# A fused transformer layer on one core: rows of v follow rows of u of the same tile by 24 beats, and the input projection runs beside the routing

## The chip, the core and the metric

One Trainium2 chip, one of its cores. The metric is the device time of one launch in microseconds; lower is better. The kernel is compared before and after one change.

## What is computed

One layer of a transformer is applied to a prompt of 1024 tokens and to 64 sample tokens (8 sequences of 8), width 1024, all in float32. For every token:

```python
qa, ka, va, qb, kb, vb, ga, gb = split(rms_norm(h, norm_mix) @ w_in)      # w_in: 1024 x 5120
o_a, o_b = attend(...)                  # branch A: difference of two softmax maps, branch B: stick-breaking
h = h + (sigmoid(ga) * (rms(o_a) @ w_proj_diff) + sigmoid(gb) * (o_b @ w_proj_sb)) @ w_out
xb = rms_norm(h, norm_ffn)
s = (xb @ w_q) against 8 heads x 2 x 128 sub-keys; top 16 of each half; top 16 of their sums -> idx, g
act = gelu(einsum('td,thkd->thk', xb, u_tab[idx]))                        # 128 rows of u for each token
h = h + einsum('thk,thkd->td', g * act, v_tab[idx])                       # 128 rows of v for each token
y = rms_norm(h, norm_final)
```

The outputs are y for prompt and sample and the keys and values of both branches. The two tables u_tab and v_tab have 16384 rows of 1024 floats. Each token takes 128 rows from each: this is most of what the kernel moves.

## The kernel before

**Stages.** A first stage makes the bias slabs and projects the first two tiles (a tile is 128 tokens, one for each partition). It ends at about 196 us. All that follows is the main stage, and the change touches only this.

**Turns and beats.** The main stage is one list of beats, written out in advance. A turn is 128 beats (`BEATS`), and in turn t the kernel attends, merges and routes for tile t (tiles 0 to 7 are the prompt, tile 8 the sample; functions `pe_piece`, `act_piece`, `dve_piece`). Beats 0 to 61 of a turn are attention. Beats 62 (`MERGE_AT`) to 84 are the merge: 24 weight blocks of 512 KB are read in order and multiplied. Beats 85 (`KEYS_AT`) to 125 are the routing, nearly all of it on VectorE, and end in the list of indices (`choose`) and the softmax gates (`gate`). TensorE, ScalarE, VectorE and GpSimd each walk the same list with a program of their own and meet at semaphores. So a wait of one engine at beat b holds all of its later beats.

**The rows.** One indirect DMA on GpSimd's queue (`pool_gather`, L1162) brings one row of u or v for each of 128 tokens, 512 KB, into one of nine places of `ring`. A place is used again once the row in it has been consumed. A row of u is multiplied with the token and summed on VectorE (`dve_dot`, L1899). A row of v is added with its weight either on VectorE (`dve_add`, L1917) or on TensorE, by a matrix product with a diagonal that ScalarE makes four beats ahead (`act_diag` L1564, `pe_add` L1388), into banks 0 and 1 of PSUM. `v_on_dve` says which. Rows of u of tile e pass in turn e+1 from beat 6 (`ULAG`); rows of v of tile e pass in turn e+2 from beat 14 (`VLAG`). In between stands one gelu over all 128 dots of the tile (L1581, turn e+2 beat 6) and one product with the gates (`dve_weights`, L1924, beat 9). The sample has 64 rows of each. The last beat is 1357.

**The end of a tile.** `dve_join` (L1930) adds the banks to the sum on VectorE, `act_finish` (L1602) and `dve_finish` (L1938) normalise it. `acc` holds three such sums.

**The projection.** Tiles 2 to 8 are projected beside the main stage, in 70 units (ten column blocks of w_in for seven tiles) of four quarters each (`pe_quarter`, L1375: two 128x512 products, four records in the trace). Each quarter has its beat: 81 in turn 0 (43 of them at beats 85 to 127), 116 in turn 1 and 83 in turn 2, at two a beat. All units of a column block follow one another, so that its weights (four loads of 512 KB, issued by ScalarE) are read once. Units go to banks 0 and 1 by turns; ScalarE takes them out and stores them (`act_quarter`, L1548). `sync_attend` and the `keys` piece of turn 3 wait until all quarters are done.

Of the kernel before, what the change touches and what calls it, by code (L numbers as in the profile page):

```python
# [48 lines left out]
R = 9  # L49
# [4 lines left out]
VLAG = 14  # L54
# [4 lines left out]
B_END = 48  # L59
# [35 lines left out]
def build(nc, a, o):  # L95
# [20 lines left out]
    with ctx:  # L116
# [138 lines left out]
        B_CHUNKS = (1, 2, 0, 4, 5, 3, 6, 7, 8, 9)  # L255
        B_UNITS = [(c, t) for c in B_CHUNKS for t in B_TILES]
# [32 lines left out]
        with ExitStack() as stage:  # L289
# [61 lines left out]
            with nc.Block() as block:  # L351
# [13 lines left out]
                def _(sp):  # L365
# [9 lines left out]
                    for j in range(4):  # L375
                        sp.dma_start(b_weights(j), b_source(B_CHUNKS[0], j)).then_inc(s_bw[j], 16)
# [219 lines left out]
        with ExitStack() as stage:  # L596
# [8 lines left out]
            acc = sb("t_acc", [P, 3, D])  # L605
# [194 lines left out]
            def row_at(beat, turns, lag):  # L800
                e, s = divmod(beat - lag, BEATS)
                return (e - turns, s) if 0 <= e - turns <= NPT and s < slots_of(e - turns) else None

            def u_at(beat):
                return row_at(beat, 1, ULAG)

            def v_at(beat):
                return row_at(beat, 2, VLAG)

            LAST_BEAT = (NPT + 2) * BEATS + VLAG + slots_of(NPT)  # L810

            def v_on_dve(e, s):

                n = slots_of(e)
                turn, b = divmod((e + 2) * BEATS + VLAG + s, BEATS)
                if (turn, b) < (FIRST, B_END):

                    return True
                if s < 3 or s >= n - 3:
                    return True  # L820
                if turn > NPT:
                    return s % 2 == 0 if b > ULAG + NS or turn > NPT + 1 else s % 3 == 0
# [118 lines left out]


            NQ = 4 * len(B_UNITS)
            quarter_beats = [b for b in range(2, MERGE_AT, 2)] + [b for b in range(MERGE_AT, KEYS_AT, 3)] + [b for b in range(KEYS_AT, BEATS)]
            quarter_beats += [BEATS + b for b in range(BEATS) if not MERGE_AT <= b < KEYS_AT or b % 2]
            left_over = NQ + 2 - len(quarter_beats)
            quarter_beats += [FIRST * BEATS + n // 2 for n in range(left_over)]
            assert quarter_beats[-1] < FIRST * BEATS + B_END
            quarters = {}
            for n, b in enumerate(quarter_beats):  # L950
                quarters.setdefault(b, []).append(n)

# [64 lines left out]
            def sync_attend(sp, t):  # L1017
                kw = width(t)
                if t >= FIRST:

                    if t >= 4:
                        sp.wait_ge(s_rmsy, t - 3)
# [29 lines left out]
                if t >= 3:  # L1052
                    sync_finish(sp, t - 3)
# [18 lines left out]
            def sync_finish(sp, e):  # L1072
                dst = y_out[1] if is_sample(e) else y_out[0][tile(e), :]
                sp.wait_ge(s_y_out, e + 1)
                sp.dma_start(dst, acc[0:out_rows(e), e % 3, :]).then_inc(s_yst, 16)

            def sync_sample(sp):
# [40 lines left out]
                for b in range(NB_DEC):  # L1118
# [13 lines left out]
                    if b == 3:  # L1132
                        sync_finish(sp, NPT - 3)
# [7 lines left out]
            def sync_program(sp):  # L1141
# [7 lines left out]
                for e in range(NPT - 2, NPT + 1):  # L1149
                    sync_finish(sp, e)  # L1150
# [46 lines left out]
            def pe_scores(pe, t, u, hf):  # L1197
                kw = width(t)
                if u == 0 and t:

                    pe.wait_ge(s_scc, 2 * t)
                if u == 0 and hf == 0:
# [164 lines left out]
            def pe_quarter(pe, n):  # L1367

                unit, j = divmod(n, 4)
                c, t = B_UNITS[unit]  # L1370
                if j == 0 and unit >= 2:
                    pe.wait_ge(s_bev, unit - 1)
                pe.wait_ge(s_bw[j], 16 * (B_CHUNKS.index(c) + 1))
                for k in range(2):
                    m = nc.tensor.matmul(ps[0:height(t), unit % 2, :], xT_of(t, 2 * j + k, 2 * j + k + 1)[:, 0, :],  # L1375
# [3 lines left out]
            def pe_add(pe, e, s):  # L1379
                n = out_rows(e)  # L1380
                if v_first(e, s):

                    pe.wait_ge(*((s_yc, e) if e else (s_bev, len(B_UNITS))))
# [8 lines left out]
            def pe_program(pe):  # L1392
                for beat in range(LAST_BEAT):
# [5 lines left out]
                    for n in quarters.get(beat, ()):  # L1399
                        if n < NQ:  # L1400
                            pe_quarter(pe, n)
                pe.wait_ge(s_fold, 1)
                pe.wait_ge(s_vsum, v_ends(NPT, True))
                for c in range(2):
                    m = nc.tensor.matmul(ps[0:NS, c, :], fold[:], acc[:, NPT % 3, c * CH:(c + 1) * CH], start=False, stop=True)
# [16 lines left out]
            def act_piece(act, t, kind, *which):  # L1422
# [113 lines left out]
            def act_quarter(act, n):  # L1536

                unit, j = divmod(n - 1, 4)
                if 0 <= unit < len(B_UNITS):
                    c, t = B_UNITS[unit]  # L1540
                    if t == B_TILES[-1] and c != B_CHUNKS[-1]:
                        act.wait_ge(s_bq, n)
                        act.dma_start(b_weights(j), b_source(B_CHUNKS[B_CHUNKS.index(c) + 1], j)).then_inc(s_bw[j], 16)
                    if j == 3:
                        act.wait_ge(s_bq, n)
                        if unit >= 2:
                            act.wait_ge(*stored(*B_UNITS[unit - 2]))
                        nc.scalar.copy(b_out(unit % 2)[0:height(t)], ps[0:height(t), unit % 2, :]).then_inc(s_bev, 1)  # L1548
                unit, j = divmod(n - 2, 4)
                if 0 <= unit < len(B_UNITS) and j == 3:  # L1550
                    c, t = B_UNITS[unit]
# [3 lines left out]
            def act_diag(act, e, s):  # L1555
                k = v_place[e, s]
                if v_first(e, s):
                    act.wait_ge(s_wgt, e + 1)
                    if is_sample(e):
                        act.wait_ge(s_fold, 1)  # L1560
# [6 lines left out]
            def act_program(act):  # L1567
                for beat in range(LAST_BEAT):
                    turn, b = divmod(beat, BEATS)
                    if b == ULAG and 1 <= turn <= NPT + 2:  # L1570
                        e = turn - 1
                        if e <= NPT and e != NPT - 1:

                            if e:
                                act.wait_ge(*dots_done(e - 1))
                            act.wait_ge(s_xn, e + 1)
                            nc.scalar.copy(both(4)[:, :], xn_of(e)).then_inc(s_xps, 1)
                        if e:
                            cols = slice(0, slots_of(e - 1))
                            act.wait_ge(*dots_done(e - 1))  # L1580
                            nc.scalar.activation(act_u[:, cols], dots[:, (e - 1) % 2, cols], ACT.Gelu).then_inc(s_gelu, 1)  # L1581
# [3 lines left out]
                    if b == VLAG and turn >= 3:  # L1585
                        act_finish(act, turn - 3)
# [3 lines left out]
                    for n in quarters.get(beat, ()):  # L1590
                        act_quarter(act, n)
                act.wait_ge(s_folded, 1)
                act_finish(act, NPT)

            def act_finish(act, e):
# [3 lines left out]
                else:  # L1599
                    act.wait_ge(s_yc, e + 1)  # L1600
                    src = acc[:, e % 3, :]
# [301 lines left out]
            def dve_add(dve, e, s):  # L1903
                total = acc[:, e % 3, :]
                if s == 0:
                    dve.wait_ge(s_h, e + 1)
                    dve.wait_ge(s_wgt, e + 1)
                if v_place[e, s]:
                    dve.wait_ge(s_vsum, v_place[e, s])
                dve.wait_ge(*arrived("v", e, s))  # L1910
# [10 lines left out]
            def dve_weights(dve, e):  # L1921
                cols = slice(0, slots_of(e))
                dve.wait_ge(s_gelu, e + 1)
                nc.vector.tensor_tensor(wgt[:, e % 2, cols], act_u[:, cols], gate[:, e % 2, cols], ALU.mult).then_inc(s_wgt, 1)  # L1924

            def dve_join(dve, e):
                total = acc[:, e % 3, :]
                dve.wait_ge(s_sum, v_ends(e, False))
                dve.wait_ge(s_vsum, v_ends(e, True))
# [78 lines left out]
```

## Time and profile before

| | |
|---|---|
| median of 3 runs | 4093.12 us (4084.87 to 4098.61) |
| profiled execution, its own time | 4105.51 us |
| its span, first to last instruction | 4103.7 us |
| TensorE busy | 3034.7 us (74%) |
| VectorE busy | 2650.3 us (65%) |
| GpSimd busy | 2373.0 us (58%) |
| ScalarE busy | 870.8 us (21%) |
| moved by DMA | 1390.19 MB, 339 GB/s over the span |

The profile is one execution. Its page gives busy times, a picture of the span in 40 slices, the chain of waits that ended last, and the costliest groups of instructions by line. Busy shares are means over stages with different limits, so the stretches below are cut at beats: the first row of u at a beat is taken from the trace (VectorE's instruction of L1899), and the time at which it starts is where that beat begins.

### The profile page before, as it was taken

What the parts mean: (1) busy time and instruction counts of PE and PEld (TensorE: products, weight loads), DVE (VectorE), ACT (ScalarE), POOL (GpSimd) and SP (SyncE); (2) the same over time, 40 slices, a digit from 0 to 9 for tenths busy, and PEclk for the clock granted to TensorE, in tenths of its full rate; (3) what the DMA queues carried; (4) which work ended last, traced back from release to release, by engine and by line L of the source; (5) the groups of instructions that cost most, each with busy time, mean ns of one, the idle gap of its engine ahead of it and who ended that gap; (6) DMA issues with size and microseconds to landing.
All of it is one profiled execution on the core that took longest, in us unless ns stands there. A gap on an engine that the chain in (4) does not pass through costs nothing.

```text
span 4103.7 us, 28498 instructions
## 1 busy us (share of the span) xinstructions
PE 3034.7 (74%) x7904; PEld 1357.0 (33%) x7904; DVE 2650.3 (65%) x5344; ACT 870.8 (21%) x1778; POOL 2373.0 (58%) x2218
## 2 busy tenths in 40 slices
PE   6899988987756776777677767776877687764566
PEld 4644433433223322332243234322432233321221
DVE  4214658675777576767676778676867665676544
ACT  4321211220122112211231123112311132111011
POOL 0100334465667566766676677656756676577776
PEclk9999999998988997889898988998989898997899
DMA  6543898899989998999899999998999999999998
GB/s 220 185 158 123 278 334 284 287 338 409 367 339 367 409 366 328 362 404 379 330 351 408 387 346 357 408 376 328 340 399 376 354 360 328 408 336 370 375 363 314
DMA packets 410545, 1390.19 MB, mean 339 GB/s; under 512 B 48493, under 2 KB 51565, under 8 KB 409197
## 3 DMA queue, kind: packets, MB, share of 16 engines
q0 software_dynamic: 316384, 1151.48, 74.5%
q1 hardware_dynamic: 74772, 200.96, 13.3%
q10 hardware_dynamic: 19232, 35.92, 2.4%
q8 instruction: 66, 1.08, 0.1%
q14 instruction: 91, 0.75, 0.0%
HBM read 1358.52 MB, written 29.66 MB: 338 GB/s over the span
## 4 chain that ended last, share of the span: by engine, by line
PE 25%; DMA 19%; POOL 16%; issue 14%; DVE 14%; another core or an unknown queue 4%; ACT 3%; SPq 0%; DVEq 0%; ACTq 0%; POOLq 0%
POOL t_ring L1162 16%; DMA t_ring<-in_peer_v,t_idx 11%; PE ps L1375 10%; PE ps L1388 5%; DVE t_ring L1899 5%; PE ps L1238 4%; DMA t_ring<-in_peer_u,t_idx 4%; DMA val<-in_w_in 2%; PE ps L1190 2%; DVE t_acc L1917 2%; PE ps L1215 1%; DMA t_big<-in_peer_w_query 1%; DMA t_big<-in_w_out 1%; DMA keyT<-in_cache_k_sb 1%
## 5 line engine op out<-in xcount | busy, mean ns | idle before, releaser
L1388 PE MATMUL ps<-t_ring,t_diag 128*128 128x512 f32 (+1 forms) x2696 | 1457.1, 672 | 613.9 <-DMA t_ring<-in_peer_v,t_idx 509.6
L1162 POOL DMA_INDIRECT t_ring<-in_peer_u,t_idx x1088 | 1153.9, 1061 | 1055.4 <-PE ps L1388 282.4
L1162 POOL DMA_INDIRECT t_ring<-in_peer_v,t_idx x1088 | 1199.5, 1102 | 497.7 <-issue 284.9
L1899 DVE CUSTOM_DVE_ANT_0 t_ring<-t_ring,ps 128x1024 f32<-128x1024 f32 x960 | 1158.2, 1214 | 379.4 <-DMA t_ring<-in_peer_u,t_idx 333.1
L1388 PEld LDWEIGHTS ps<-t_ring,t_diag 128*128 128x128 f32 (+1 forms) x2696 | 509.6, 207 | 1460.8 <-DMA t_ring<-in_peer_v,t_idx 886.6
L1917 DVE SCALAR_TENSOR_TENSOR t_acc<-t_ring,t_wgt,t_acc 128x1024 f32<-128x1024 f32 x413 | 531.1, 1286 | 194.5 <-DMA t_ring<-in_peer_v,t_idx 163.5
L1238 PE MATMUL ps<-t_big,t_pTr 128*128 128x512 f32 x864 | 428.1, 641 | 92.5 <-DMA t_big<-in_w_out 24.6
L1564 ACT ACTIVATE t_diag<-ident,t_wgt 128x128 f32<-128x128 f32 x645 | 248.9, 400 | 893.2 <-PE ps L1388 489.3
L1375 PE MATMUL ps<-val,keyT 128*128 128x512 f32 x800 | 368.8, 604 | 29.6 <-DMA val<-in_w_in 28.5
L1416 ACT COPY t_pTr<-ps 128x512 f32<-128x512 f32 (+3 forms) x216 | 111.1, 514 | 800.9 <-PE ps L1190 525.2
L1238 PEld LDWEIGHTS ps<-t_big,t_pTr 128*128 128x128 f32 x864 | 166.6, 203 | 338.1 <-issue 187.1
L1375 PEld LDWEIGHTS ps<-val,keyT 128*128 128x128 f32 x800 | 149.2, 193 | 200.6 <-issue 168.2
L1899 DVE CUSTOM_DVE_ANT_0 t_ring<-t_ring,t_xn_sb 128x1024 f32<-128x1024 f32 x128 | 156.1, 1221 | 53.1 <-DMA t_ring<-in_peer_u,t_idx 48.8
L1215 PE MATMUL ps<-keyT,t_big 128*128 128x512 f32 (+3 forms) x384 | 169.7, 556 | 22.1 <-DVE t_mx L1628 10.0
L1190 PE MATMUL ps<-ident,t_big 128*128 128x128 f32 x576 | 101.7, 291 | 100.3 <-ACT t_pTr L1416 40.6
L1628 DVE CUSTOM_DVE_ANT_0 t_big<-ps,t_big 128x128 f32<-128x128 f32 (+7 forms) x64 | 48.4, 756 | 178.9 <-PE ps L1215 85.7
L1375 PE MATMUL ps<-val,xT_end 128*128 128x512 f32 (+1 forms) x320 | 144.9, 596 | 0.0
L1228 PEld LDWEIGHTS ps<-val,t_pTr 128*128 128x128 f32 x864 | 119.9, 206 | 69.5 <-issue 59.0
L1190 PEld LDWEIGHTS ps<-ident,t_big 128*128 128x128 f32 x576 | 72.1, 150 | 177.8 <-issue 93.0
L1228 PE MATMUL ps<-val,t_pTr 128*128 128x64 f32 (+1 forms) x864 | 117.4, 284 | 15.7 <-ACT t_pTr L1416 8.3
L1215 PEld LDWEIGHTS ps<-keyT,t_big 128*128 128x128 f32 x384 | 75.3, 214 | 94.8 <-issue 79.7
L1548 ACT COPY val<-ps 128x512 f32<-128x512 f32 (+1 forms) x70 | 41.0, 586 | 304.8 <-PE ps L1375 290.3
(215 smaller groups left out, 2177.8 us busy)
## 6 DMA issues: line engine op xcount, KB each, us to landing
t_big<-in_w_out SPq DMA_DIRECT2D x72, 512.0 KB
t_big<-in_peer_w_query SPq DMA_DIRECT2D x72, 512.0 KB
wraw<-in_w_in SPq DMA_DIRECT2D x40, 512.0 KB, 5.9
t_big<-in_w_proj_diff SPq DMA_DIRECT2D x36, 512.0 KB
val<-in_w_in ACTq DMA_DIRECT2D x36, 512.0 KB
t_big<-in_w_proj_sb SPq DMA_DIRECT2D x36, 512.0 KB
t_ring<-in_peer_u,t_idx POOLq DMA_INDIRECT x1088
t_ring<-in_peer_v,t_idx POOLq DMA_INDIRECT x1088
```

The lines of the kernel that those rows point to most:

```text
L1162: pool.indirect_dma_start(row(kind, e, s), None, table, bass.IndirectOffsetOnAxis(ap=idx[:, e % 3, s:s + 1], axis=0)).then_inc(s_ring[g % ...
L1190: m = nc.tensor.transpose(ps[:, 6, k * P:k * P + n], blk, ident[0:n, 0:n])
L1215: m = nc.tensor.matmul(scores_of(t, hf)[:, c:c + wide], qz[:, u, hf, :], keyT[:, u, c:c + wide], start=True, stop=True)
L1228: m = nc.tensor.matmul(ps[:, 7, col:col + wide], pTr[:, kb, :], val[:, kb, u * P + hf * 64:u * P + hf * 64 + wide], start=(kb == 0), stop= ...
L1238: m = nc.tensor.matmul(ps[:, 2 + c, :], pTr[:, k, :], wring[:, w % 4, c * CH:(c + 1) * CH], start=(k == blocks[0]), stop=(k == blocks[1] - 1))
L1375: m = nc.tensor.matmul(ps[0:height(t), unit % 2, :], xT_of(t, 2 * j + k, 2 * j + k + 1)[:, 0, :], b_weights(j)[:, k, :], start=(j == 0 and ...
L1388: m = nc.tensor.matmul(ps[0:n, c, :], diag[:, v_place[e, s] % NDG, 0:n], row("v", e, s)[:, c * CH:(c + 1) * CH], start=v_first(e, s), stop ...
L1416: act_T.raised_by(nc.scalar.copy(dst, src))
L1564: nc.scalar.activation(diag[:, k % NDG, 0:out_rows(e)], unit[:], ACT.Copy, scale=wgt[:, e % 2, s:s + 1]).then_inc(s_diag, 1)
L1628: nc.vector.tensor_tensor_reduce(out=z_of(u)[:, hf, 0:kw], in0=scores_of(t, hf), in1=bias[:, u % 2, 0:kw], scale=1.0, scalar=LOWEST, op0=A ...
L1899: nc.vector.tensor_tensor_reduce(out=row("u", e, s), in0=row("u", e, s), in1=x_row, scale=1.0, scalar=0.0, op0=ALU.mult, op1=ALU.add, accu ...
L1917: m = nc.vector.scalar_tensor_tensor(out=total, in0=row("v", e, s), scalar=wgt[:, e % 2, s:s + 1], in1=total, op0=ALU.mult, op1=ALU.add)
```

## The change

The four numbers and the planning of beats change, and what hangs on them:

- Rows of v of tile e pass in turn e+1, 24 beats behind the rows of u of the same tile. They were a turn and eight beats behind. The last beat is 1245 in place of 1357.
- Gelu and the product with the gates are made for groups of 16 rows, two and three beats after the group's last dot.
- `acc` holds two sums in place of three, and `ring` has ten places in place of nine.
- Quarters: 64 in turn 0 (26 of them from beat 85), 112 in turn 1, 104 in turn 2, the last at beat 116. Between beats 85 and 127 of turns 1 and 2 they go to banks 2 and 3, since banks 0 and 1 then hold the sum of v; at each passage from one pair of banks to the other the first quarter waits.
- The column blocks 6 to 9 come first for tile 2 alone and then for tiles 3 to 8, so each is read twice: 14 sets of weights in place of 10.
- Rows of v in turn 1, and in turn 2 up to beat 84, are added on VectorE, but for two of three at beats 85 to 123 of turn 1. The join of tile 0 stands at beat 2 of turn 2, that of a later tile at beat 30 of the next turn but one.

```diff
-R = 9
+R = 10
-VLAG = 14
+VLAG = 24
+GROUP = 16
+JOIN_0 = 2
-        B_CHUNKS = (1, 2, 0, 4, 5, 3, 6, 7, 8, 9)
-        B_UNITS = [(c, t) for c in B_CHUNKS for t in B_TILES]
+        B_GROUPS = [(c, B_TILES) for c in (1, 2, 0, 4, 5, 3)]
+        B_GROUPS += [(c, B_TILES[:1]) for c in (6, 7, 8, 9)] + [(c, B_TILES[1:]) for c in (6, 7, 8, 9)]
+        B_UNITS = [(c, t) for c, tiles in B_GROUPS for t in tiles]
...
-            acc = sb("t_acc", [P, 3, D])
+            acc = sb("t_acc", [P, 2, D])
...
             def v_at(beat):
-                return row_at(beat, 2, VLAG)
+                return row_at(beat, ULAG + VLAG)
+            def group_at(beat, lag):
+                row = row_at(beat, ULAG + GROUP - 1 + lag)
+                return (row[0], row[1] // GROUP) if row and row[1] % GROUP == 0 else None
+            def weighed(e, g):
+                return e * (NSLOT // GROUP) + g + 1
-            LAST_BEAT = (NPT + 2) * BEATS + VLAG + slots_of(NPT)
+            LAST_BEAT = (NPT + 1) * BEATS + ULAG + VLAG + slots_of(NPT)
...
+            quarter_beats = [b for b in range(2, MERGE_AT, 2)] + [b for b in range(MERGE_AT, KEYS_AT, 3)] + [b for b in range(KEYS_AT, KEYS_AT + 26)]
+            quarter_beats += [BEATS + b for b in range(MERGE_AT)] + [BEATS + b for b in range(MERGE_AT + 1, MERGE_AT + 20, 2)]
+            quarter_beats += [BEATS + b for b in range(KEYS_AT, KEYS_AT + 40)]
+            quarter_beats += sorted([2 * BEATS + b for b in range(JOIN_0 + 1, MERGE_AT)] + [2 * BEATS + b for b in (20, 30, 40)])
+            quarter_beats += [2 * BEATS + b for b in range(MERGE_AT + 1, MERGE_AT + 20, 2)] + [2 * BEATS + b for b in range(KEYS_AT, KEYS_AT + 32)]
+            def bank_of(unit):
+                return 2 * beside_routing(unit) + unit % 2
...
             def v_on_dve(e, s):
...
-                if (turn, b) < (FIRST, B_END):
-                    return True
+                if turn == 1 or e == 0 or (turn == 2 and b < KEYS_AT):
+                    return not (turn == 1 and KEYS_AT <= b < BEATS - 4) or s % 3 == 0
...
-                return b < MERGE_AT and s % 3 == 0
+                return (b < MERGE_AT or turn == 2) and s % 3 == 0
...
             def pe_quarter(pe, n):
+                if j == 0 and beside_routing(unit) and not beside_routing(unit - 2):
+                    pe.wait_ge(s_scc, 2 * turn + 2)
+                if j == 0 and unit >= 2 and beside_routing(unit - 2) and not beside_routing(unit):
+                    pe.wait_ge(s_yc, 1)
...
+            def act_gelu(act, e, g):
+                cols = slice(g * GROUP, (g + 1) * GROUP)
+                act.wait_ge(s_dot, e * NSLOT + (g + 1) * GROUP)
+                if e:
+                    act.wait_ge(s_wgt, weighed(e - 1, g))
+                nc.scalar.activation(act_u[:, cols], dots[:, e % 2, cols], ACT.Gelu).then_inc(s_gelu, 1)
...
-            def dve_weights(dve, e):
-                cols = slice(0, slots_of(e))
-                dve.wait_ge(s_gelu, e + 1)
+            def dve_weights(dve, e, g):
+                cols = slice(g * GROUP, (g + 1) * GROUP)
+                dve.wait_ge(s_gelu, weighed(e, g))
                 nc.vector.tensor_tensor(wgt[:, e % 2, cols], act_u[:, cols], gate[:, e % 2, cols], ALU.mult).then_inc(s_wgt, 1)
...
+                    if group_at(beat, 2):
+                        act_gelu(act, *group_at(beat, 2))
...
-                    if b == ULAG + 3 and 2 <= turn:
-                        dve_weights(dve, turn - 2)
+                    if group_at(beat, 3):
+                        dve_weights(dve, *group_at(beat, 3))
```

## Rows read from the trace of the kernel before

**Rows 1.** The page: busy times by engine; DMA's rate in 40 slices.

```profile
PE 3034.7 (74%) x7904; PEld 1357.0 (33%) x7904; DVE 2650.3 (65%) x5344; ACT 870.8 (21%) x1778; POOL 2373.0 (58%) x2218
...
GB/s 220 185 158 123 278 334 284 287 338 409 367 339 367 409 366 328 362 404 379 330 351 408 387 346 357 408 376 328 340 399 376 354 360 328 408 336 370 375 363 314
```

**Rows 2.** Busy time by stretch: us, each engine's busy us (instructions), PE clock, DMA share, GB/s.

```profile
1566.10:1980.10 414.00, 292.85 (x744) 131.22 (x744) 290.79 (x591) 89.22 (x192) 269.38 (x256) 0.88 0.96 368
3909.30:4062.40 153.10, 101.57 (x203) 30.26 (x204) 75.55 (x62) 22.14 (x57) 114.54 (x105) 0.96 0.97 367
4062.40:4103.70 41.30, 19.22 (x34) 4.28 (x32) 15.56 (x13) 2.10 (x5) 20.75 (x16) 0.84 0.65 225
```

**Rows 3.** The chain that ended last, 384 to 760 us: start, us, what.

```profile
383.76 29.33 PE ps L1375 x68
...
659.89 15.36 DMA val<-in_w_in
675.29 38.19 PE ps L1375 x88
```

**Rows 4.** VectorE in order of time, 378 to 430 us: start, us, instruction.

```profile
384.52 0.29 DVE L1832 TENSOR_TENSOR t_gate<-t_gexp,t_grec 128x128 f32<-128x128 f32 x1
418.37 0.43 DVE L1628 CUSTOM_DVE_ANT_0 t_big<-ps,t_big 128x256 f32<-128x256 f32 x1 [33.55 <-PE ps L1215]
```

**Rows 5.** As rows 2: turn 1 from beat 30, cut at beats 62, 85, 127.

```profile
474.00:537.20 63.20, 59.10 (x168) 27.01 (x167) 43.25 (x81) 11.82 (x25) 30.02 (x32) 1.00 0.90 334
537.20:612.80 75.60, 60.23 (x146) 25.76 (x145) 32.91 (x51) 8.00 (x13) 20.01 (x23) 0.95 0.88 321
612.80:725.00 112.20, 98.79 (x244) 42.05 (x242) 92.74 (x299) 13.79 (x21) 47.70 (x43) 0.98 0.85 294
725.00:751.10 26.10, 23.54 (x61) 10.73 (x60) 10.28 (x26) 6.68 (x13) 7.52 (x8) 1.00 0.75 285
```

**Rows 6.** As rows 2: turn 2 from beat 6, cut at beats 30, 62, 85.

```profile
751.10:842.30 91.20, 89.97 (x251) 40.28 (x249) 59.83 (x105) 25.17 (x54) 46.65 (x40) 1.00 0.85 292
842.30:947.40 105.10, 81.30 (x208) 35.93 (x207) 72.86 (x103) 16.85 (x36) 68.03 (x62) 0.89 0.94 353
947.40:1035.80 88.40, 69.00 (x168) 30.08 (x166) 56.49 (x71) 11.82 (x22) 51.76 (x48) 0.92 1.03 408
1035.80:1159.00 123.20, 85.54 (x169) 29.40 (x168) 95.65 (x298) 18.82 (x45) 83.06 (x83) 0.97 0.96 362
```

**Rows 7.** As rows 2: turn 3 and the boundary before it, the same cuts.

```profile
1159.00:1190.90 31.90, 18.25 (x44) 8.39 (x42) 14.31 (x27) 8.14 (x15) 15.66 (x16) 0.73 0.71 267
1190.90:1262.60 71.70, 44.55 (x135) 21.96 (x136) 59.76 (x106) 27.58 (x61) 53.09 (x48) 0.87 0.97 376
1262.60:1357.10 94.50, 66.30 (x167) 29.71 (x166) 60.84 (x92) 16.89 (x37) 65.09 (x65) 0.83 0.98 377
1357.10:1447.30 90.20, 64.85 (x166) 27.83 (x164) 56.47 (x70) 13.42 (x25) 49.67 (x49) 0.98 1.03 408
1447.30:1570.40 123.10, 90.63 (x167) 31.48 (x168) 95.54 (x298) 17.21 (x42) 83.95 (x82) 0.92 0.96 358
```

**Rows 8.** The costliest groups: a row of v added on VectorE.

```profile
L1917 DVE SCALAR_TENSOR_TENSOR t_acc<-t_ring,t_wgt,t_acc 128x1024 f32<-128x1024 f32 x413 | 531.1, 1286 | 194.5 <-DMA t_ring<-in_peer_v,t_idx 163.5
```

**Rows 9.** ScalarE in order of time around a gelu, 744 to 760 us.

```profile
750.01 1.02 ACT L1577 COPY ps<-t_xn_sb 128x1024 f32<-128x1024 f32 x1
...
751.05 1.28 ACT L1581 ACT_TABLE_LOAD   x1
752.34 0.31 ACT L1581 ACTIVATE t_act_u<-t_dots 128x128 f32<-128x128 f32 x1
752.67 1.28 ACT L1441 ACT_TABLE_LOAD   x1
```

**Rows 10.** GpSimd's waits in turn 4: who for whom, us in total, times, longest.

```profile
POOL t_ring L1162 <- issue: 65.0, 209, 1.1
POOL t_ring L1162 <- PE ps L1388: 50.4, 15, 11.3
POOL t_ring L1162 <- remote: 20.3, 9, 3.5
```

More of the change, by code:

```diff
@@ L798, in slots_of, with row_at @@
                 return NSLOT // 2 if e == NPT else NSLOT
-            def row_at(beat, turns, lag):
-                e, s = divmod(beat - lag, BEATS)
-                return (e - turns, s) if 0 <= e - turns <= NPT and s < slots_of(e - turns) else None
+            def row_at(beat, lag):
+                e, s = divmod(beat - BEATS - lag, BEATS)
+                return (e, s) if 0 <= e <= NPT and s < slots_of(e) else None
             def u_at(beat):
-                return row_at(beat, 1, ULAG)
+                return row_at(beat, ULAG)
@@ new lines, in build, with beside_routing @@
+            quarter_beats += [2 * BEATS + b for b in range(MERGE_AT + 1, MERGE_AT + 20, 2)] + [2 * BEATS + b for b in range(KEYS_AT, KEYS_AT + 32)]
+            assert len(quarter_beats) == NQ
+            quarters = {}
+            for n, b in enumerate(quarter_beats):
+                quarters.setdefault(b, []).append(n)
+            def beside_routing(unit):
+                turn, b = divmod(quarter_beats[4 * unit], BEATS)
+                ends = divmod(quarter_beats[4 * unit + 3], BEATS)
+                assert not turn or (turn, b >= KEYS_AT) == (ends[0], ends[1] >= KEYS_AT)
+                return turn > 0 and b >= KEYS_AT
@@ L939, in build @@
                 at(KEYS_AT + 40, "gate", of=pieces)
[L943 to L951, printed above, removed]
             def unit_of(c, t):
@@ L1148, in sync_program @@
                 sync_weights(sp, NPT)
-                for e in range(NPT - 2, NPT + 1):
+                for e in range(NPT - 1, NPT + 1):
                     sync_finish(sp, e)
@@ L1556, in act_diag @@
                 k = v_place[e, s]
[L1557 to L1560, printed above, removed]
+                if s == min(r for r in range(s // GROUP * GROUP, slots_of(e)) if not v_on_dve(e, r)):
+                    act.wait_ge(s_wgt, weighed(e, s // GROUP))
+                if v_first(e, s) and is_sample(e):
+                    act.wait_ge(s_fold, 1)
                 if k >= NDG:
@@ L1569, in act_program @@
                     turn, b = divmod(beat, BEATS)
-                    if b == ULAG and 1 <= turn <= NPT + 2:
+                    if b == ULAG and 1 <= turn <= NPT + 1 and turn != NPT:
                         e = turn - 1
[L1572 to L1577, printed above, removed]
                         if e:
-                            cols = slice(0, slots_of(e - 1))
                             act.wait_ge(*dots_done(e - 1))
-                            nc.scalar.activation(act_u[:, cols], dots[:, (e - 1) % 2, cols], ACT.Gelu).then_inc(s_gelu, 1)
+                        act.wait_ge(s_xn, e + 1)
+                        nc.scalar.copy(both(4)[:, :], xn_of(e)).then_inc(s_xps, 1)
+                    if group_at(beat, 2):
+                        act_gelu(act, *group_at(beat, 2))
                     ahead = v_at(beat + DIAG_AHEAD)
@@ L1589, in act_program @@
                         act_piece(act, t, *piece)
-                    for n in quarters.get(beat, ()):
+                    for n in quarters.get(beat - 2, ()):
+                        act_store(act, n)
+                    for n in quarters.get(beat - 1, ()):
                         act_quarter(act, n)
```

111 lines of the change are left out of this document (64 added, 47 removed).

## Prediction

> **What bounds the kernel now.** I read the page first: no engine is above 74%, but from turn 2 on DMA moves 340 to 409 GB/s in nearly every slice, against 158 to 334 in the slices before [rows 1]. Then I cut the span at beats. In turn 4, a steady one, 256 rows pass in 414.0 us, 1.62 us a row, with DMA at 0.96 and 368 GB/s [rows 2]. The merge of turn 3 runs at 408 GB/s with DMA's share at 1.03 [rows 7]; I take 408 as the roof. At it the 152 MB of a steady turn (414.0 x 368) would take 373 us, so a turn is transfer with some 40 us of gaps, and rows cost about the same wherever they stand, if the engines keep up.
>
> The two ends are different. From beat 62 of turn 9 on 152 rows are left and almost nothing stands beside them: 105 pass in 153.1 us, 1.46 us each [rows 2]. At the other end turn 1 has one row a beat, and DMA is not full: 334, 321, 294 and 285 GB/s [rows 5]. There the chain of waits runs through quarters on TensorE, not through rows: 68 records of L1375 in 29.33 us, 88 in 38.19 [rows 3]. Four records are a quarter: 1.73 us. So the kernel is bound by TensorE in turns 0 to 2 and by transfer after that, and the change moves 112 rows from the second kind of stretch to the first: 98 into turn 1, 14 into turn 2, all off the end.
>
> **End of turn 0.** VectorE finishes the gates at 384.8 us and has nothing until 418.4: 33.55 us for the scores of tile 1 [rows 4], and in that time the chain holds 68 records, 17 quarters, in 29.33 us [rows 3]. These are the backlog: 43 quarters stand at beats 85 to 127. The change leaves 26, just 17 fewer. TensorE would be done at 383.8 and VectorE waits for the short chain of transposes alone. Removed: **-29**. This is no transfer-bound stretch, so nothing else is late next; the 17 return below.
>
> **The end.** Beats from 62 of turn 9 on: 40 rows in place of 152. 112 x 1.46 = **-163**. The last 41.3 us with their sums and stores [rows 2] stay.
>
> **Turn 1.** For each stretch I take the traffic it had, add 0.524 MB for each new row and divide by the rate that turn 3 shows at the same beats; then I look whether an engine needs more. A row of v costs VectorE 1.29 us [rows 8]; on TensorE it has the same two products as a quarter, 1.73.
> - Beats 6 to 30: no row of v, the same quarters: 0.
> - 30 to 62: 63.2 us x 334 = 21.1 MB, plus 32 rows (16.8) = 37.9, at 377 [rows 7] 100 us. VectorE 43.3 + 32 x 1.29 = 85, TensorE 59 [rows 5]. 100: +37.
> - 62 to 85: 24.3 + 12.1 = 36.3 MB at 408: 89 us, +13. TensorE has one quarter less.
> - 85 to 127: 33.0 MB + 42 rows (22.0) + eight extra weight loads (4.2: units 42 and 43 are alone in their groups) = 59.2. At 358 [rows 7] 165 us, at 408 145. TensorE 98.8 + 26 rows - 2 quarters = 140; VectorE 92.7 + 17 x 1.29 = 115. 152, between the two rates, nearer the roof as this mix has big loads: +40.
> - 127 to 6: 31.9 as in turn 3 [rows 7], and 2 for weights: +8.
>
> Sum **+98**. The rest of GpSimd's queue behind these rows is only more rows.
>
> **Turn 2.**
> - 6 to 30: TensorE 90.0 - 23 quarters (40) = 50. VectorE 59.8 + 8 x 1.29 = 70. Traffic 26.6 MB + 8 rows (4.2) + eight loads (4.2) - 3.6 for 23 quarters' weights and stores = 31.4, at 376 84 us: -7 [rows 6, 7].
> - 30 to 62: 11 quarters more, 10 rows fewer on TensorE (83 us), VectorE 86; traffic 37.1 + 1.7 = 38.8 MB at 377: 103: -2.
> - 62 to 85: 36.1 + 1.6 MB at 408: +4.
> - 85 to 127: 44.6 + 4.9 MB, 121 to 138 us; TensorE 85.5 + 32 quarters - 14 rows = 117; VectorE 95.7 + 14 x 1.29 = 114. 134: +11.
>
> Sum **+6**. That the last quarter comes at beat 116, and SyncE's loads for turn 3 stand behind it, leaves about 12 beats at 2.95 us, 35 us, for 1 MB; cost nothing. If the quarters run that late, all of turn 3 starts later, one to one.
>
> Bounds for both turns together: with 408 GB/s in every stretch about 45 less, +60. With nothing hidden, each moved row and quarter paid on its engine one after the other: turn 1 72 x 1.29 + 26 x 1.73 less 4 quarters, plus 8.4 MB at 377, +153; turn 2 (37 rows more on VectorE, 29 fewer and 30 quarters more on TensorE) +50. So +60 to +203; I take +104, since TensorE and VectorE stay under the transfer time in all stretches.
>
> **Steady turns, 3 to 8.** The same 256 rows, the same shares of the engines. Two small terms.
>
> *Gelu in groups.* The trace has one per tile: table load 1.28, gelu 0.31, and then 1.28 again for the table of exp [rows 9]. The seven more bring by my reading of the beats some seven loads and seven gelus, 10.6 us of ScalarE a turn, which has 89 of 414 busy [rows 2]. Behind ScalarE's wait stand its copies for TensorE's transposes and the diagonals; behind VectorE's wait for the gelu stand the dots that free the ring. VectorE has two beats of its own work between the last dot and the product, TensorE four beats after that, and a beat lasts 2.95 us (94.5 / 32 [rows 7]). Bounds: 0, and all 10.6. The product on 16 columns is not in the trace; below the 0.28 of 128. I take +3 a turn. The Trainium skill, page "ScalarE: Activation LUTs", section "What ACT_TABLE_LOAD costs", gives 1.28 us for the load and 1.38 more for a drain, 2.66 for each switch. The trace agrees on the load and shows no drain: copy until 751.03, load at 751.05, gelu at 752.34, next load at 752.67 [rows 9]. By the page ScalarE would have 20 us more a turn, by the rows 10.6.
>
> *The tenth place.* GpSimd issues a row when a place is free. In turn 4 it waits 15 times for TensorE, 50.4 us in all, and 9 times for something unseen, 20.3 us [rows 10]. With one place more, one more row is under way at each such wait. 24 x 1.46 = 35 us is the upper bound, 0 the lower; what is full at 408 gives nothing back, and the longest wait, 11.3 us, is mended by an eighth. I take -6.
>
> Together -3 a turn, six turns: **-18**.
>
> **Sum.** -29 - 163 + 98 + 6 - 18 = -106. The span goes from 4103.7 to 3998, the execution's own time from 4105.5 to 3999.5. The median of the runs was 4093.12, 0.9970 of that execution: 3987 us.
>
> **The rivals.**
>
> *The ring gives more.* If half of the 35 us of each steady turn comes back and the gelus cost nothing, -17 a turn in place of -3: another 84, 3903 us. For it: the waits are few and long. Against: the floor of 373 us a turn, and that a place more doesn't make TensorE's own waits shorter. 0.10.
>
> *The first turns take it all.* If in turns 1 and 2 nothing is hidden, +203 meets -192 and the steady terms take off what is left: 4086 us, with the steady terms at nothing 4104; no change. For it: in turn 1 TensorE is at 94% of beats 30 to 62 and VectorE waits on it for each score; five changes of weights follow one another at units 41 to 46, and the chain showed 15.36 us for such a load [rows 3], where four beats are 12. Against: 74 to 123 GB/s of unused rate there [rows 5]. 0.12.
>
> *Slower: each group of 16 stops the ring.* VectorE must have a group's gelu before it goes on, ScalarE must have the dots before it copies anything for TensorE. If the load, the gelu and the load back (2.87 us [rows 9]) show in full for each of the 59 added gelus, that is +169: -29 - 163 + 104 + 169 = +81, 4174 us. It decides from 88 / 59 = 1.5 us a group on, about one load and the gelu. For it: ScalarE is already held for long stretches in its own order. Against: the beats between, and that rows wait for transfer anyway. 0.13. By the page's switch of 2.66 us the group would cost 5.6 us, +332, 4335 us; the trace agrees only with the load of 1.28.
>
> **How the numbers follow.** My forecast, 3987, has 0.62, with a range of its own of 3935 to 4040 from the bounds of the first two turns and of the steady terms; the rivals 0.10, 0.12 and 0.13, 0.03 for the rest. The range of 3900 to 4085 leaves out the slower rival, a part of the no-change one, and the fastest tail. Within 0.3% (12 us) is what a measurement of this kernel can hardly tell from no change. Faster: 0.62 + 0.10 + half of the second rival, 0.78. Same 0.08, slower 0.14.
>
> **What would show it.** In the trace after: the wait of VectorE before tile 1's first scores shrinks from 33.6 us to under 8. Turn 1 lasts about 425 us from beat 6 to beat 6, not 324, with DMA at 360 or more from beat 30; turn 2 about 445. Turns 3 to 7 keep 409 to 414 us. From beat 62 of turn 9 to the end 70 us in place of 233. Wrong it would be if VectorE's or TensorE's rows show waits for ScalarE's gelu of over 1.5 us each, if turn 1 is over 500 us, or if steady turns move by over 10 us.

## The result, and the profile after

The kernel after the change takes 3972.07 us (median of four runs, 3960.66 to 3981.93). The kernel before, on the same chip, takes 4088.99 us (four runs, 4071.45 to 4098.61). The ratio is 0.9718, with a 95% interval of 0.9673 to 0.9763: 2.8% faster. The forecast was 3987 us, with a chance of 0.78 for faster. The profiled execution took 3976.95 us, its span 3975.2.

The page after the change, busy times and DMA's rate in 40 slices, beside [rows 1]:

```profile
PE 2933.8 (74%) x7680; PEld 1324.0 (33%) x7680; DVE 2721.1 (68%) x5459; ACT 923.5 (23%) x1836; POOL 2399.5 (60%) x2218
...
GB/s 217 201 143 128 339 410 407 397 406 410 409 374 361 387 402 354 344 375 408 365 337 347 409 388 323 348 404 407 311 358 386 377 344 384 356 359 354 344 375 323
```

TensorE has 101 us less to do and VectorE 71 more: 56 rows of v went from the one to the other. What matters is DMA's rate in the fifth to tenth slices: 278, 334, 284, 287, 338 and 409 GB/s before, 339, 410, 407, 397, 406 and 410 now.

VectorE in order of time, after, between the gates of tile 0 and the first scores of tile 1 (start, us, instruction, in brackets the idle time before it):

```profile
385.02 0.29 DVE L1880 TENSOR_TENSOR t_gate<-t_gexp,t_grec 128x128 f32<-128x128 f32 x1
391.31 0.42 DVE L1676 CUSTOM_DVE_ANT_0 t_big<-ps,t_big 128x256 f32<-128x256 f32 x1 [6.00 <-PE ps L1245]
```

The wait of 33.55 us [rows 4] is 6.00.

Busy time by stretch, after; the columns are those of [rows 2]. The first five lines are turn 1 from beat 6, cut at beats 30, 62, 85 and 127 as in [rows 5]; the next five are turn 2 with the same cuts, as [rows 6] and the first line of [rows 7]; then turn 4 as in [rows 2]; then beats 30 to 62 of turn 9, and all that follows:

```profile
399.60:452.50 52.90, 47.50 (x139) 22.27 (x138) 38.20 (x91) 18.09 (x47) 21.79 (x24) 1.00 0.86 316
452.50:556.50 104.00, 82.55 (x219) 36.59 (x217) 83.44 (x115) 18.83 (x35) 71.09 (x64) 0.92 1.01 390
556.50:640.10 83.60, 61.35 (x148) 27.12 (x149) 62.67 (x77) 10.24 (x18) 50.84 (x47) 0.87 1.03 409
640.10:775.90 135.80, 122.01 (x286) 49.26 (x284) 114.91 (x318) 22.76 (x47) 92.43 (x85) 0.99 1.02 399
775.90:802.20 26.30, 14.40 (x27) 6.30 (x28) 21.29 (x32) 6.77 (x10) 15.73 (x15) 0.74 1.03 406
802.20:879.20 77.00, 60.53 (x171) 28.59 (x170) 68.29 (x114) 21.14 (x49) 51.66 (x46) 0.93 1.03 408
879.20:983.90 104.70, 79.37 (x207) 35.00 (x206) 86.79 (x117) 23.24 (x39) 72.70 (x66) 0.87 1.03 408
983.90:1071.90 88.00, 69.51 (x164) 29.86 (x162) 62.71 (x78) 10.31 (x18) 50.34 (x47) 0.90 1.03 410
1071.90:1200.30 128.40, 113.22 (x248) 45.25 (x248) 112.05 (x316) 20.65 (x47) 89.42 (x83) 0.95 0.99 382
1200.30:1229.20 28.90, 18.75 (x46) 8.59 (x46) 13.24 (x26) 9.11 (x17) 15.45 (x16) 0.76 0.78 300
...
1637.00:2050.40 413.40, 288.25 (x746) 128.77 (x745) 291.63 (x597) 99.22 (x206) 272.13 (x257) 0.89 0.96 369
3817.40:3905.10 87.70, 46.03 (x75) 11.90 (x76) 58.18 (x85) 10.65 (x28) 63.22 (x62) 0.79 1.01 389
3905.10:3975.20 70.10, 38.22 (x70) 9.33 (x68) 31.81 (x35) 6.77 (x18) 37.59 (x37) 0.85 0.77 290
```

Read the last number of each line. From beat 62 of turn 1 to beat 85 of turn 2 all stretches but one stand at 406 to 410 GB/s with DMA's share at 1.03, where before they had 285 to 353 (408 in the merge of turn 2 alone). The one is turn 1's beats 85 to 127, at 399 GB/s. So these 515 us stand at or near the roof. The whole account, between the same beats:

| stretch | before | after | change | forecast |
|---|---|---|---|---|
| up to the first row of u | 427.0 | 399.6 | -27.4 | -29 |
| turn 1 | 324.1 | 402.6 | +78.5 | +98 |
| turn 2 | 439.8 | 427.0 | -12.8 | +6 |
| turns 3 to 8 | 2524.0 | 2521.2 | -2.8 | -18 |
| turn 9, beats 6 to 62 | 155.9 | 154.7 | -1.2 | 0 |
| from there to the end | 232.9 | 70.1 | -162.8 | -163 |
| sum | 4103.7 | 3975.2 | -128.5 | -106 |

(A turn goes from its beat 6 to the next turn's.)

### The profile page after: what moved, and what is told of

It reads as the page before. It is cut to its first block, busy times and chain, and to the rows that moved or that the text cites. A ratio compares the mean times of both kernels' runs of the same rounds, so it can differ in the third digit from the quotient of the medians.

```text
span 3975.2 us, 28361 instructions
## 1 busy us (share of the span) xinstructions
PE 2933.8 (74%) x7680; PEld 1324.0 (33%) x7680; DVE 2721.1 (68%) x5459; ACT 923.5 (23%) x1836; POOL 2399.5 (60%) x2218
## 4 chain that ended last, share of the span: by engine, by line
DMA 21%; PE 19%; POOL 19%; issue 15%; DVE 14%; ACT 3%; another core or an unknown queue 3%; SPq 0%; DVEq 0%; ACTq 0%; POOLq 0%
POOL t_ring L1189 19%; DMA t_ring<-in_peer_v,t_idx 13%; PE ps L1268 6%; DVE t_ring L1947 5%; PE ps L1428 5%; PE ps L1412 3%; DMA t_ring<-in_peer_u,t_idx 3%; DMA t_big<-in_w_out 2%; DMA t_big<-in_peer_w_query 2%; PE ps L1217 2%; DVE t_acc L1968 2%; PE ps L1245 1%; DMA keyT<-in_cache_k_sb 1%; PE ps L1258 1%
## 5 line engine op out<-in xcount | busy, mean ns | idle before, releaser
L1428 PE MATMUL ps<-t_ring,t_diag 128*128 128x512 f32 (+1 forms) x2472 | 1338.3, 672 | 516.5 <-DMA t_ring<-in_peer_v,t_idx 442.1
L1189 POOL DMA_INDIRECT t_ring<-in_peer_u,t_idx x1088 | 1209.5, 1112 | 682.8 <-issue 268.2
L1189 POOL DMA_INDIRECT t_ring<-in_peer_v,t_idx x1088 | 1170.4, 1076 | 713.7 <-issue 310.0
L1428 PEld LDWEIGHTS ps<-t_ring,t_diag 128*128 128x128 f32 (+1 forms) x2472 | 467.1, 206 | 1255.8 <-DMA t_ring<-in_peer_v,t_idx 740.2
L1968 DVE SCALAR_TENSOR_TENSOR t_acc<-t_ring,t_wgt,t_acc 128x1024 f32<-128x1024 f32 x469 | 603.6, 1287 | 152.6 <-DMA t_ring<-in_peer_v,t_idx 125.8
L1268 PE MATMUL ps<-t_big,t_pTr 128*128 128x512 f32 x864 | 440.7, 655 | 113.1 <-DVE t_big L1750 43.8
L1412 PE MATMUL ps<-val,keyT 128*128 128x512 f32 x800 | 390.0, 624 | 57.9 <-DMA val<-in_w_in 46.5
L1605 ACT ACTIVATE t_diag<-ident,t_wgt 128x128 f32<-128x128 f32 x583 | 222.7, 398 | 577.4 <-PE ps L1428 294.0
L1245 PE MATMUL ps<-keyT,t_big 128*128 128x512 f32 (+3 forms) x384 | 161.7, 534 | 23.4 <-issue 10.2
```

The costliest lines, as they stand in the source:

```text
L1189: pool.indirect_dma_start(row(kind, e, s), None, table, bass.IndirectOffsetOnAxis(ap=idx[:, e % 3, s:s + 1], axis=0)).then_inc(s_ring[g % ...
L1245: m = nc.tensor.matmul(scores_of(t, hf)[:, c:c + wide], qz[:, u, hf, :], keyT[:, u, c:c + wide], start=True, stop=True)
L1268: m = nc.tensor.matmul(ps[:, 2 + c, :], pTr[:, k, :], wring[:, w % 4, c * CH:(c + 1) * CH], start=(k == blocks[0]), stop=(k == blocks[1] - 1))
L1412: m = nc.tensor.matmul(ps[0:height(t), bank_of(unit), :], xT_of(t, 2 * j + k, 2 * j + k + 1)[:, 0, :], b_weights(j)[:, k, :], start=(j == ...
L1428: m = nc.tensor.matmul(ps[0:n, c, :], diag[:, v_place[e, s] % NDG, 0:n], row("v", e, s)[:, c * CH:(c + 1) * CH], start=v_first(e, s), stop ...
L1605: nc.scalar.activation(diag[:, k % NDG, 0:out_rows(e)], unit[:], ACT.Copy, scale=wgt[:, e % 2, s:s + 1]).then_inc(s_diag, 1)
```

## The experiments

All change the kernel after. The first four were compared with the kernel before on one chip, the last three on another. The kernel after itself was not run on the second chip, so the last three are held against it by their ratios to the kernel before; spans of theirs are compared across chips.

**The same kernel again**, as the base for the others.

> The changed kernel again, timed on the chip of the three runs beside it, as what they are held against. All theories: 0.972 of the kernel before.

Measured: 3966.99 us, ratio 0.9702 (0.9683 to 0.9721), span 3965.2. Up to the first row of u 401.1, turn 1 401.5, turn 2 435.0, turns 3 to 8 2502.1, the end 68.8. So the account above repeats within 2 us, but for turn 2, which moves by 8 between two profiles of one kernel, and the sum of turns 3 to 8, which moves by 19. A difference of some us a steady turn can't be read from two profiles; for that the ratios must serve.

**Nine places in the ring again.**

```diff
-R = 10
+R = 9
```

> The changed kernel with nine places in the ring in place of ten. Turns 3 to 8 came out only 2.8 us shorter in all, where I had forecast 18. Theory A (two real terms that cancel: the tenth place gives 6 us a turn or more, the gelus in groups take nearly as much): 6 us a turn and about 50 us in all slower than the changed kernel. Theory B (the tenth place gives next to nothing, since the waits of the ring come from engines that stand still longer than a row's pace): under 10 us in all.

Measured: 3974.72 us, ratio 0.9704 (0.9682 to 0.9725), as without the edit. Turn 4 lasts 412.3 us with ten places, 409.9 with nine. GpSimd's waits in that turn, ten places (who for whom, us in total, times, longest):

```profile
POOL t_ring L1189 <- issue: 67.8, 214, 1.8
POOL t_ring L1189 <- PE ps L1428: 39.2, 14, 9.3
POOL t_ring L1189 <- DVE t_dots L1947: 14.8, 19, 3.7
POOL t_ring L1189 <- remote: 14.3, 7, 3.3
```

The same view with nine:

```profile
POOL t_ring L1189 <- issue: 74.0, 229, 2.6
POOL t_ring L1189 <- PE ps L1428: 37.6, 11, 9.2
POOL t_ring L1189 <- remote: 13.0, 5, 3.3
POOL t_ring L1189 <- DVE t_dots L1947: 11.5, 13, 3.3
```

Apart from "issue" that is 68.3 us with ten places and 62.1 with nine, in as long a turn. A place more does not shorten the waits for a consumer. The 6 us a turn that I took for it would be 36 us here; the ratios differ by 0.0002, 1 us, with an interval of some 11 us to either side for the difference. The rival "the ring gives more" falls with them.

**Groups of eight**, twice the gelus and more changes of table.

```diff
-GROUP = 16
+GROUP = 8
```

> Groups of 8 rows in place of 16: 68 more gelus, with their table loads where another function stands between, 64 more products with the gates. Theory A (each added gelu takes 0.4 us of the time, as 3 us a turn for seven): 25 to 30 us slower. Theory B (ScalarE's idle time hides them): within 10 us of the changed kernel. The slower rival of the prediction (2.87 us for each gelu): 190 us slower.

Measured: 3963.65 us, ratio 0.9701 (0.9680 to 0.9722): no change. ScalarE's groups of instructions for the gelu, groups of 16 (count, busy us, mean ns, idle us before):

```profile
L1640 ACT ACT_TABLE_LOAD x48 | 61.6, 1283 | 6.8 <-PE ps L1412 5.3 <-ACT val L1587 0.5 <-issue 0.3
...
L1640 ACT ACTIVATE t_act_u<-t_dots 128x16 f32<-128x16 f32 x68 | 14.6, 215 | 102.8 <-DVE t_dots L1947 64.7 <-issue 24.0 <-remote 13.4
```

And groups of eight:

```profile
L1640 ACT ACT_TABLE_LOAD x72 | 92.4, 1283 | 4.6 <-PE ps L1412 2.3 <-issue 0.7 <-ACT val L1587 0.4
...
L1640 ACT ACTIVATE t_act_u<-t_dots 128x8 f32<-128x8 f32 x136 | 28.3, 208 | 211.5 <-DVE t_dots L1947 115.5 <-issue 69.9 <-remote 22.4
```

The line charges ScalarE with 44.5 us more (30.8 for the loads, 13.7 for the gelus). With 15 more loads on other lines ScalarE as a whole is busy 983.4 us in place of 922.3, and the median is 3 us shorter. The slower rival needed 1.5 us for each added group, 102 us for these 68; it is refuted. One thing is easier here than in the kernel after: a group of eight leaves ten beats between its product with the gates and its first diagonal, a group of 16 two. Two more things to see. Only 48 of 68 gelus, and 72 of 136, had to load the table: the others found it in place. And ScalarE idles 102.8 and 211.5 us before its gelus, most of it for the last dot of the group: the gelu is early, not late. VectorE's product with the gates, which needs the gelu, shows no wait for it in the kernel after (idle before the 68 products, us and times):

```profile
L1975 DVE TENSOR_TENSOR t_wgt<-t_act_u,t_gate x68: 151/164/224, 435.9 to 3933.9; 128x16 f32<-128x16 f32 x68
...
  issue: 1.0, 2
```

**The backlog back in turn 0**: 16 quarters from beats 101 to 116 of turn 2 into beats 111 to 126 of turn 0; each quarter between takes an earlier beat.

```diff
-... + [b for b in range(KEYS_AT, KEYS_AT + 26)]
+... + [b for b in range(KEYS_AT, KEYS_AT + 42)]
...
-... + [2 * BEATS + b for b in range(KEYS_AT, KEYS_AT + 32)]
+... + [2 * BEATS + b for b in range(KEYS_AT, KEYS_AT + 16)]
```

> The changed kernel, but 42 quarters at the routing beats of turn 0 in place of 26, as nearly as before the change, and 16 fewer at the routing beats of turn 2. Theory A (the backlog of TensorE holds tile 1's first scores, and in turn 2 the quarters lie beside transfer): VectorE's first row of u comes 16 x 1.73 = 28 us later, turn 2's beats 85 to 127 shorten by 0 to 8 us, total 20 to 28 us slower. Theory B (a quarter costs its 1.73 us wherever it stands): no change in all.

Measured: 3982.63 us, ratio 0.9734 (0.9711 to 0.9757), 13 us slower than its base by the ratios (with some 12 to either side), 20.8 by the spans. The first row of u comes at 426.1 us, not 401.1. Busy time by stretch, with the backlog: turn 1 beats 6 to 30, turn 2 beats 85 to 127:

```profile
426.10:471.60 45.50, 45.50 (x139) 23.41 (x138) 38.20 (x91) 17.89 (x47) 21.75 (x24) 1.00 0.90 306
...
1094.40:1220.40 126.00, 90.95 (x184) 35.54 (x184) 112.06 (x317) 17.71 (x42) 88.68 (x82) 0.89 0.97 368
```

The same stretches of the base:

```profile
401.10:452.90 51.80, 48.72 (x139) 22.87 (x138) 38.22 (x91) 18.19 (x47) 21.77 (x24) 0.97 0.88 322
...
1072.80:1202.80 130.00, 115.48 (x247) 44.85 (x245) 112.29 (x317) 20.12 (x45) 91.09 (x84) 0.93 0.99 376
```

Look at the last: TensorE has 24.5 us less to do there, and the stretch is 4.0 us shorter. In turn 0 sixteen quarters cost 25.0 us, 1.56 each. Within turn 1, where the quarters only take earlier beats, gains and losses cancel (401.1 us in place of 401.5): beats 85 to 127 last 143.5 us for 135.5. A quarter is at nearly its full price where all wait for it and nearly free where rows are being transferred. That is the first term of the forecast, confirmed by undoing it.

**The transposes of the keys ahead.** A steady turn begins with a gap that the forecast passed over: from beat 127 to beat 6 DMA has 267 GB/s in [rows 7] and 300 after the change. TensorE in order of time there, base kernel, the start of turn 5:

```profile
2026.43 0.60 PE L1217 MATMUL ps<-ident,gain_mix 128*128 128x128 f32 x4
2034.45 1.12 PE L1217 MATMUL ps<-ident,gain_mix 128*128 128x128 f32 x4 [7.43 <-ACT keyT L1455]
```

ScalarE at the same time:

```profile
2033.81 0.58 ACT L1455 COPY keyT<-ps 128x512 f32<-128x512 f32 x1 [17.02 <-remote]
```

The transposes end at 2027.03 and the copy that waits for them starts at 2033.81. What the wait costs is seen in DMA: during it the places of the ring are filled at full rate, and then DMA runs dry: VectorE's last dot ends at 2029.7, and no row is consumed until TensorE's product at 2044.05. Busy time in and after the wait, same run:

```profile
2027.10:2034.00 6.90, 0.00 (x0) 0.00 (x0) 2.42 (x3) 0.19 (x1) 2.95 (x4) 0.74 1.03 409
2034.00:2044.00 10.00, 5.97 (x16) 3.66 (x17) 0.00 (x0) 5.37 (x9) 3.67 (x4) 0.50 0.74 256
2044.00:2048.00 4.00, 4.00 (x7) 1.65 (x6) 3.58 (x8) 1.61 (x4) 0.08 (x1) 0.56 0.00 0
```

The edit moves this piece of tile t from beat 0 of its turn to beat 122 of the turn before, on both engines.

```diff
-            at(0, "keys")
+            at(122, "keys")
...
                 if kind == "keys":
-                    if t >= FIRST:
+                    t = t + 1
+                    if FIRST <= t < NPT:
```

> The changed kernel, but the transposes of the next tile's keys stand at beat 122 of the turn before in place of beat 0. Ring and gelus being free, what holds the steady turns is open. Theory C (the 32 us of the seven beats around each turn's start are a serial chain, key transposes, query transposes, scores, and 10 to 12 us of it are the keys' part, 8 of them a wait between TensorE's last key transpose and its signal): each of the seven turn starts 2 to 8 gets 8 to 12 us shorter, 50 to 80 us in all. Theory D (transfer sets the turns, and what a turn start loses the rest makes up; or the 8 us wait moves with the transposes): under 15 us.

Measured: 3945.87 us, ratio 0.9608 (0.9574 to 0.9642), span 3941.0: the fastest of all, faster than both kernels of the case. ScalarE's copy, now at the end of turn 4:

```profile
1997.72 0.58 ACT L1456 COPY keyT<-ps 128x512 f32<-128x512 f32 x1 [6.77 <-issue]
```

TensorE there:

```profile
1997.03 0.60 PE L1217 MATMUL ps<-ident,gain_mix 128*128 128x128 f32 x4
```

The 6.8 us between transposes and copy are gone. Beats 127 to 6 at the start of turn 5, with the edit:

```profile
2007.70:2032.70 25.00, 19.31 (x46) 8.83 (x45) 14.02 (x25) 8.90 (x15) 16.90 (x17) 0.86 0.97 364
```

and in the base:

```profile
2020.70:2054.90 34.20, 22.04 (x54) 10.60 (x53) 14.03 (x25) 9.97 (x17) 17.16 (x17) 0.75 0.74 271
```

Over the six starts, turns 3 to 8, 190.8 us (192.1 in the first profile of the same kernel) become 154.8, 36.0 less. Turn 8 has no such piece and hardly moves (25.2 to 24.2), and neither does turn 2 (26.3 to 26.4), where the copy came 1.07 us after the transposes before the edit too. The gain is that of turns 3 to 7, and it goes with the delay between transposes and copy:

| turns 3 to 7 | starts, sum | delays, sum | starts less delays |
|---|---|---|---|
| base | 165.6 | 31.7 | 133.9 |
| the same kernel, first profile | 167.2 | 29.6 | 137.6 |
| nine places | 150.7 | 19.0 | 131.7 |
| keys ahead | 130.6 | 0.4 | 130.2 |

(With the keys ahead the piece stands before beat 127, and so outside these stretches; beats 111 to 127 of turns 2 to 6 last 223.4 us in all, in the base 224.2.) The piece can come without a delay at beat 0 too: at turn 3's start it is 0.09 us in the first profile and 8.04 in the base, and the start lasts 28.9 us and 34.8.

By the spans 24.2 us of the 36.0 are left; by the ratios it is 39 us, with some 16 to either side. Both expectations missed: the gap was neither all path nor covered by something else. Where the rest goes is open: beats 85 to 111 of turns 3 to 7 last 410.1 us in all with the edit and 394.3 in the base, but 403.9 in the first profile of the base's kernel.

**Rows of v 16 beats behind.**

```diff
-VLAG = 24
-GROUP = 16
+VLAG = 16
+GROUP = 8
```

> Groups of 8 and rows of v 16 beats behind those of u in place of 24. Eight rows move off the end, where one costs 1.46 us, into beats 22 to 29 of turn 1, where DMA has 316 GB/s of 408: the working of the prediction gives 12 us off the end and up to 4 added in turn 1, 8 to 12 us faster than the changed kernel. If ScalarE's and VectorE's two beats between a group's gelu and its first diagonal are too few, turns 3 to 8 grow instead, 10 us or more in all.

Measured: 3987.08 us, ratio 0.9706 (0.9671 to 0.9742). The end gives what was worked out, but beats 6 to 30 of steady turns take it back. Over turns 4 to 7 these last 324.2 us in all, in the base 286.0 and in the first profile of the same kernel 281.1. The edited kernel, turn 5 beats 6 to 30, and the end from beat 62 of turn 9:

```profile
2057.20:2137.80 80.60, 54.93 (x186) 31.66 (x185) 64.04 (x108) 36.56 (x71) 53.64 (x48) 0.79 0.93 341
...
3923.70:3981.80 58.10, 30.96 (x52) 7.34 (x52) 26.63 (x33) 4.87 (x12) 28.40 (x27) 0.79 0.73 272
```

The base there:

```profile
2054.90:2127.20 72.30, 56.04 (x198) 31.62 (x196) 59.09 (x101) 29.31 (x63) 55.53 (x49) 0.91 0.99 374
...
3896.40:3965.20 68.80, 36.31 (x70) 8.68 (x68) 31.80 (x35) 6.18 (x16) 36.88 (x36) 0.88 0.79 293
```

The end is 10.7 us shorter for eight rows, 1.3 each, and turns 3 to 8 are 33.5 longer (2535.6 against 2502.1). Against the first profile of the same kernel turns 3 to 8 are 14.4 longer. By the ratios the two cancel. A wait in those beats that the base has at 2.3 us (who for whom, us in total, times, longest):

```profile
PE ps L1217 <- ACT t_pTr L1455: 13.0, 1, 13.0
```

The sums of the tile before are joined and normalised at beat 22 then, amid attention's branch A, not at beat 30. Whether that place is the cause or the lag of 16 itself stays open. The two beats between product and first diagonal were the expectation's reason for such a loss, but they hold all through a turn, and beats 30 to 62 of turns 4 to 7 are no longer than in the base (379.9 us in all against 386.3). Groups of eight cost nothing at a lag of 24, with ten beats there; at 16 they were not tried apart from the lag.

**Both together**, keys ahead and 16 beats.

> Both of the edits of the two runs before in one kernel: the sum of their effects, by theory C 60 to 90 us faster than the changed kernel, by theory D 5 to 25.

Measured: 3962.24 us, ratio 0.9642 (0.9604 to 0.9680). The turn starts are as short as with the keys alone (23.7 to 27.7 us in turns 3 to 8), beats 6 to 30 of turns 4 to 7 as long as with the short lag alone (80 to 87 us). The two effects stand side by side; the keys alone are best.

## Why the prediction was right, and where its sizes were off

The total came nearer than its terms. In the first profile turns 1 and 2 came out 38.3 us under the forecast and turns 3 to 8 15.2 over it; that these partly cancel is luck. The mechanism, rows of v into transfer that stood idle and quarters out of a stretch in which all waited for them, holds.

*End of turn 0* (-29, measured -27.4): right, by the wait of VectorE and by the run that undid it.

*The end* (-163, measured -162.8): right. 112 rows at 1.46 us each. Its pace has one more reason than was given: in [rows 2] GpSimd is busy 114.5 us with 105 rows and needs 0.3 us between two of them, 146 of the 153.1 us. So by these rows it is the issuing of rows that paces this end more than the transfer, which stood at 367 GB/s and not at 408; no run tested it. GpSimd's rows in the chain of waits after the change, turn 1 (start, us):

```profile
480.02 0.94 POOL t_ring L1189
481.27 1.31 POOL t_ring L1189
```

0.94 us for a row and 0.31 until the next: 1.25 us at best. The sum was right since it took the measured pace and not a rate.

*Turn 1* (+98, measured +78.5): the mechanism was right (DMA fills up, TensorE and VectorE stay under it), the term of beats 85 to 127 was mis-sized: +40 forecast, 112.2 to 135.8, +23.6, measured. I had chosen 152 us between two rates, with 59.2 MB. The stretch moved 54.2 MB (135.8 x 399); at 399 GB/s my 59.2 MB would have been 148 us. So some 4 us of the 16 were the rate, the rest the bytes. The eight extra weight loads are there. What is missing is mostly traffic of SyncE's queue (q1), which the stretch had before: two blocks of query weights and the reads of keys and values are issued before beat 85 now. The stretch before, 612.8 to 725.0 (packets, MB, share; loads of w_in issued):

```profile
q1 hardware_dynamic: 1857, 4.07, 9.5%
...
val<-in_w_in ACTq DMA_DIRECT2D x8, 512.0 KB
```

And after, 640.1 to 775.9:

```profile
q1 hardware_dynamic: 576, 0.72, 1.5%
...
val<-in_w_in ACTq DMA_DIRECT2D x16, 512.0 KB
```

That is 3.4 of the 5.0 MB; rows brought 21.0 MB more in place of 22.0, and ScalarE's queue (weights and stores) 3.6 in place of 4.2. The other stretches: 30 to 62 +40.8 for +37, 62 to 85 +8.0 for +13, 127 to 6 +0.2 for +8. Beats 6 to 30 were put at 0 and cost +5.9. The chain of waits has a load of weights there:

```profile
430.48 12.33 DMA val<-in_w_in
```

With the backlog back in turn 0 the same beats last 45.5 us, TensorE is busy for all of them, and the chain there has no such load.

*Turn 2* (+6, measured -12.8; -4.8 in the second run of the same kernel): again the rate. For beats 6 to 30 31.4 MB at 376 were to give 84 us; 31.4 MB did pass (77.0 x 408), at the roof, in 77.0. The steady turns' rates at the same beats were the wrong yardstick: a stretch can be held below the roof there by something that the first turns don't have. What that is was not tried. Of the 18.8 us by which turn 2 stayed under its forecast 7 are in these beats, 6 in beats 85 to 127 (128.4 us for 134), 4 in the merge, and 3 at turn 3's start, with 2 too much in beats 30 to 62. At that start this profile has no delay between transposes and copy and the kernel before has 8.41 us.

*Steady turns* (-18, measured -2.8 and, in the second run of the same kernel, -21.9): the sum can't be judged by the profiles, but its terms can by the runs that undid or doubled them. The tenth place, -6 a turn, and the gelus, +3 a turn, changed nothing when they were undone and doubled, each within some 11 us over the whole kernel. So no run shows either of them; what is left of the steady turns' change is no more than the scatter from profile to profile (19 us).

*The rivals.* "The first turns take it all" would have needed +203 in turns 1 and 2; they took +65.7. The weight changes at beats 85 to 127 of turn 1 did not stop the list of beats: the chain of waits has none of their loads there. The other two fell with the ring and the groups.

The prediction also priced the slower rival by the Trainium skill, page "ScalarE: Activation LUTs", section "What ACT_TABLE_LOAD costs": with a drain of 1.38 us beside each load of 1.28, +332 us. The runs agree on the load (1283 ns) and show no drain in the time: 68 more gelus with 24 more loads on their own line cost nothing. By the page's 2.66 us for a switch these 24 alone would be 64 us of ScalarE, as an estimate; ScalarE's own busy time grew by 61.1 us for all 39 added loads and the 68 gelus together.

## What to carry over

Move work from where it stands alone at the end of a kernel to where the shared resource is idle, and price it there by bytes over the roof, not by the mean rate of some other stretch; the engines only have to stay under that time. A small compute piece is nearly free beside transfers and costs its full length in a stretch where an engine waits for it. Before adding a buffer, look at what ends the waits of its producer: if it is the consumer's own pace, a place more may buy nothing, as here.

## What was not expected of the hardware

- **One core's DMA holds 406 to 410 GB/s for long**, not only in a merge: 296 us in a row from 775.9 on, with gathered rows of 4 KB as the main part. The Trainium skill, page "HBM Reference", section "Specifications (TRN2)", has about 358 GB/s per core and says that a core which streams alone gets more; the runs, with one core, agree with the second.
- **A signal up to 10 us late.** At the starts of turns 3 to 7 ScalarE's copy follows TensorE's transposes by 4.79 to 10.01 us in nine of ten cases (two profiles of the same kernel) and by 0.09 in the tenth; with the piece at beat 122 by 0.09 in all five. It isn't the transposes alone. GpSimd, which waits for a place that TensorE's row product before them frees, goes on only at the same moment:

```profile
2033.94 0.93 POOL L1189 DMA_INDIRECT t_ring<-in_peer_v,t_idx  x1 [3.34 <-remote]
```

  The key rows for the transposes were asked for 148 us earlier (1878.62). So what is late is on TensorE's side, its work or its record; which of the two was not settled.
- **The clock after a short idle.** TensorE's granted clock was 1.00 before that wait (2020.0 to 2027.2 us). It stood idle from 2027.03 to 2034.45, and from 2034.0 to 2044.0 the granted clock is 0.50, with matmul groups at half the pace: four transposes take 0.60 us before and 1.12 after. That is the lower of its two levels, 1.2 in place of 2.4 GHz.
